# A decoder layer on one core: who makes the rests of the two down weight pieces of the third product

## The reference, cut to what matters

```python
z = rmsnorm(h, norm_mlp[l])                                   # h: 1024 x 1024
h = h + jnp.square(jax.nn.relu(z @ w_up[l])) @ w_down[l]      # w_up 1024 x 4096, w_down 4096 x 1024
return rmsnorm(h, norm_final)
```

## Time and profile before

| | |
|---|---|
| runs, median of 3 | 1497.07 us (1497.02 to 1497.55) |
| profiled execution, its own time | 1496.87 us |
| its span, first to last instruction | 1494.8 us |
| TensorE clock granted, mean | 0.995 |
| busy: PE, DVE, ACT, POOL | 98%, 66%, 35%, 35% |
| a window (seven of them, the last 500 us or so) | 77.6 to 77.7 us |

### The profile page before, as it was taken

The page is one execution under the profiler, slowest core; times in us unless marked ns, Lnnn a source line. Parts: engine busy times, 40 slices in busy tenths (PEclk is TensorE's granted clock), DMA queues, the critical chain, the costliest instruction groups (busy, mean ns, idle before and its releaser), DMA issues.

```text
span 1494.8 us, 20639 instructions
## 1 busy us (share of the span) xinstructions
PE 1465.8 (98%) x7019; PEld 1210.5 (81%) x7019; DVE 981.0 (66%) x1911; ACT 517.9 (35%) x1003; POOL 519.2 (35%) x349
## 2 busy tenths in 40 slices
PE   9999999999999999999999999999999999999995
PEld 8887888888888888888888888878787878787874
DVE  6898564543467527675624788595958586767678
ACT  7422312400122212241101322545444444444455
POOL 4000001245332332004333003273737373646556
PEclk9999999999999999999999999999999999999998
DMA  7225543282111101003542001333333333333333
GB/s 221 99 90 143 144 109 124 72 279 88 57 43 43 43 29 57 29 29 131 179 176 71 1 29 50 120 99 116 103 112 106 104 108 107 108 107 110 107 111 135
DMA packets 150933, 149.02 MB, mean 100 GB/s; under 512 B 19104, under 2 KB 109904, under 8 KB 150864
## 3 DMA queue, kind: packets, MB, share of 16 engines
q1 hardware_dynamic: 118048, 107.00, 23.2%
q10 hardware_dynamic: 32816, 41.12, 8.5%
HBM read 126.58 MB, written 21.50 MB: 99 GB/s over the span
## 4 chain that ended last, share of the span: by engine, by line
PE 84%; DVE 9%; issue 3%; ACT 2%; POOL 1%; ACTq 1%; DMA 0%; DVEq 0%; POOLq 0%
PE acc L799 19%; PE acc L801 19%; PE acc L800 19%; PE aux L800 7%; PE aux L801 7%; PE aux L799 7%; DVE h_ring L2602 1%; DVE h_res L2634 1%; PE aux L1081 1%; PE aux L1074 1%; PE aux L1084 1%; DVE h_sum L2609 1%; PE aux L964 1%; PE aux L958 0%; PE aux L1069 0%
## 5 line engine op out<-in xcount | busy, mean ns | idle before, releaser
L799 PE MATMUL acc<-z_hi,w_hi 128*128 128x512 f32 x448 | 177.2, 396 | 0.6 <-DVE z_lo L1874 0.6
L801 PE MATMUL acc<-z_hi,w_lo 128*128 128x512 f32 x448 | 174.6, 390 | 0.0
L800 PE MATMUL acc<-z_lo,w_hi 128*128 128x512 f32 x448 | 174.5, 390 | 0.0
L799 PE MATMUL acc<-w_hi,z_hi 128*128 128x512 f32 x384 | 164.4, 428 | 0.0
L801 PE MATMUL acc<-w_hi,z_lo 128*128 128x512 f32 x384 | 150.5, 392 | 0.0
L800 PE MATMUL acc<-w_lo,z_hi 128*128 128x512 f32 x384 | 149.6, 390 | 0.0
L663 POOL CAST w_hi<-stage 128x1024 fp32r<-128x1024 f32 x22 | 27.7, 1259 | 344.2 <-PE acc L801 290.0
L650 POOL TENSOR_SCALAR stage<-stage,nm 128x512 f32<-128x512 f32 x48 | 78.3, 1643 | 168.8 <-PE acc L801 86.0
L767 POOL TENSOR_TENSOR t_raw<-t_raw,p_a 128x512 f32<-128x512 f32 x28 | 39.5, 1409 | 262.3 <-DMA p_a<-in_w_up 157.1
L799 PEld LDWEIGHTS acc<-z_hi,w_hi 128*128 128x128 f32 x448 | 84.1, 188 | 19.8 <-issue 1.5
L801 PEld LDWEIGHTS acc<-z_hi,w_lo 128*128 128x128 f32 x448 | 84.1, 188 | 17.9
(11 more groups left out here) (417 smaller groups left out, 3879.7 us busy)
## 6 DMA issues: line engine op xcount, KB each, us to landing
stage<-in_w_in SPq DMA_DIRECT2D x28, 512.0 KB, 4.4
p_a<-in_w_up SPq DMA_DIRECT2D x56, 256.0 KB, 2.8
p_a<-in_w_down SPq DMA_DIRECT2D x56, 256.0 KB, 2.6
gate_dram<-gate_t ACTq DMA_DIRECT2D x32, 256.0 KB, 2.1
p_b<-in_w_up SPq DMA_DIRECT2D x28, 256.0 KB, 2.7
p_b<-in_w_down SPq DMA_DIRECT2D x28, 256.0 KB, 2.7
x_in<-in_x SPq DMA_DIRECT2D x8, 512.0 KB, 6.1
stage<-in_w_in SPq DMA_DIRECT2D x32, 128.0 KB, 2.3
```

What stands on the lines that cost most here:

```text
L799: nc.tensor.matmul(out, s_hi, m_hi_, start=first, stop=False, skip_group_check=partial)
L800: nc.tensor.matmul(out, s_hi, m_lo_, start=False, stop=False, skip_group_check=partial)
L801: return nc.tensor.matmul(out, s_lo, m_hi_, start=False, stop=last, skip_group_check=partial)
```

## The change

VectorE instead of GpSimd makes the rests of pieces 18 and 19 of every window.

```diff
--- before
+++ after
@@ -69,7 +69,7 @@
 N_PROD = len(PRODUCTS)
 PIECES, RING, HRING = 4 * N_PROD, 7, 3
 UP_PIECES = 2 * N_PROD
-V_PIECES = range(3, 18)
+V_PIECES = range(3, 20)
 SUMS = 16
```

## The result

The changed kernel takes 1505.52 us (median of six, 1504.24 to 1506.49) against 1497.16 us for the one before (six, 1496.98 to 1497.55). The ratio is 1.0054, with a 95% interval of 1.0042 to 1.0067: slower by 8.4 us, where 6.5 us (1503.4 us) was predicted. The profiled execution took 1506.17 us, its span is 1504.1 us.

What follows compares the result with a forecast made beforehand. PE, busy 98%, bounds the kernel; only its idle time before piece 18 can change. Chain steps 0.85 + 1.30 - 0.14 - 1.09 = 0.92 us a window, 6.5 in seven: 1496.87 + 6.5 = 1503.4 us, range 1498.0 to 1508.0.

Steps and rivals of the forecast that it cites:

- What PE waits for: Before piece 18, PE idles 1.15 us for DVE's hidden_lo(4), not for the rests that the change moves.
- about 2.0: Sign in the changed kernel: PE's wait before piece 18 in us, instead of 1.15, still ended by hidden_lo(4).
- the slip before piece 17: hidden_lo(3) ends 0.2 us later than PE wants it for piece 17; the wait at piece 18 swallows this.
- Step 1, sum 21: POOL's sum 21 starts earlier, takes its turn behind hidden_s3(1) and ends 1.15 us after it.
- Step 2: DVE's hidden_s1(1) waits for sum 21, ending 0.55 us behind it and 0.97 us later than before.
- Step 4: DVE's rest 18, issued at 1136.24, waits for POOL's rest 20 and is done at 1137.62.
- Steps 5 and 6: POOL's sum 22 goes before hidden_s2(1)'s end; hidden_lo(4) then has no POOL turn ahead and takes 0.69 us.
- The sum: PE starts piece 18 0.92 us later in each window, 6.5 us in seven.
- No gap opens before piece 19: hidden_lo(5) ends by about 1141.2, or 1142.3 with one more POOL turn; PE wants it at 1142.78.
- A: Rival: POOL's operations fall beside add_pair or into DVE's gaps; piece 18 0.58 us earlier per window, 1492.8 us; chance 0.12.
- B: Rival: sum 21 after hidden_lo(3), sum 22 in front of hidden_lo(4); 0.6 us later per window, 1501 us; chance 0.10.
- C: Rival: POOL also gets in front of hidden_lo(4), 1.15 us more per window, 14.5 us in all, 1511.4 us; chance 0.05.

Runs made afterwards that it cites:

- Experiment 4: Kernel before, nothing moved, GpSimd waits with rest 19 and all behind it until hidden_lo(4) is done: 1493.04 us, ratio 0.997.
- Experiment 5: Changed kernel, with GpSimd waiting with sum 21 and all behind it until hidden_lo(4) is done: 1499.08 us, ratio 1.0011 against the kernel before.
- experiment 3: Changed kernel, with GpSimd's sum 21 also waiting for ScalarE's cast 18: 1508.64 us, ratio 1.0074 against the kernel before.
- experiment 1: Kernel before with only rest 18 moved to VectorE, rest 19 left on GpSimd: 1511.73 us, ratio 1.0104.
- experiments 1 to 7: The follow-up kernels, variants of the kernel before or the changed one in moved rests, GpSimd waits or a repeated hidden_lo(4): 1492.81 to 1534.47 us.

## Why the prediction was right

The direction and the term that carries it held, and the mechanism showed step by step:

- *What PE waits for.* `hidden_lo(4)`, not the rests that are moved. Experiment 4 shows it: taking GpSimd out of its way, PE's gap falls from 1.30 to 0.20 us. The two waits put down to POOL's `t_b` in the earlier trace rows went with the others. In the changed kernel the idle time before piece 18 is 1.82 us where "about 2.0" stood: the slip before piece 17 is taken from it.
- *Step 1, sum 21.* Predicted to start behind `hidden_s3(1)`; its data was there 2.77 us after the issue (2.82 expected), and it ends 1.15 us after `hidden_s3(1)`, as worked out.
- *Step 2.* `hidden_s1(1)` predicted at 1.66 us, measured 1.67. PE's slip before piece 17 was predicted at 0.2 us and is 0.25 with the slow matmul behind it; the gap that follows swallows it, as said.
- *Step 4.* Rest 18 predicted at 1.38 us, measured 1.38.
- *Steps 5 and 6.* `hidden_s2(1)` 0.65 and 0.68 us; `hidden_lo(4)` 0.69 and 0.68 us.
- *The sum.* 0.92 us a window predicted, 0.95 measured; 6.5 and 6.7 us in seven. No gap opens before piece 19, as said.

**The term that was missing** is the clock. The prediction priced PE's longer wait at its length alone, and said that a change outside PE can win or lose only PE's idle time. But behind a gap of 2 us the granted clock sometimes falls to half for eight matmuls, 0.2 us lost on each, 1.6 us a time, and this is time in which PE is busy (78.44 instead of 76.79 us in the window). It is in none or one of the six whole windows of the changed kernel's three traces. That fits the spread of the six timed executions, 2.2 us where the kernel before had 0.6 beside them. The rest of the difference is in the early part and isn't the change's. 8.4 us were measured where 6.7 + 1.6 x (0 to 1) + 0 to 1.0 stands.

**The rivals.** A (1492.8 us) asked that sum 21's data land over 1.5 us later than it did; the trace of the changed kernel speaks against it, and its own condition, GpSimd's operations beside the `add_pair` ones, wasn't made in any run. Experiment 5, which takes GpSimd out of the chain by holding it, gives 1499.1: the gap is A's, and a late GpSimd costs the rest behind it. B was priced at 4 us and said to lie in the range; experiment 3, which is close to it, costs 11 us, in good part by the wait before piece 19 that I hadn't worked out. So had the data of sum 21 landed some 1.3 us later, the forecast of 6.5 us would have been 4 to 5 us too low by experiment 3, an estimate: the number leaned on one landing time, and that was read rightly. C's extra turn in front of `hidden_lo(4)` is there in experiment 1, where rest 18 waits less in exchange: 0.56 us more a window than the change (gaps of 2.54 and 1.98 us), not the 1.15 that I had put on it.

The Trainium skill (SBUF — State Buffer, Who interferes with whom) says of the shared pair that the one who issues first holds it for its whole instruction. The ends in every trace here agree, with a blocked VectorE operation 0.55 us behind GpSimd's end and about 1.15 us the other way. The same page's Summary: rules for kernel authors advises to schedule whichever is off the critical path. Experiment 4 is a way to do so, and there it is worth 4.5 us.

## What to carry to other kernels

Moving an operation from GpSimd to VectorE doesn't take GpSimd out of VectorE's way: its next instruction moves up and takes the turn, and the moved one lengthens VectorE's own chain. Find the VectorE operation that TensorE waits for, and hold GpSimd back there with a wait, if what it would do isn't due yet (here one wait, 4.5 us faster, where the move cost 8.4), and hold it no longer than that: experiment 5 held it 6.3 us and lost behind the gap what it had won there. When a chain is worked out turn by turn, go on to the next two places where TensorE could wait, and price each gap of TensorE with the clock that may follow it.

## What the runs showed of the hardware

- Half clock behind a gap, which I had not expected of gaps this short: matmuls 0.43 us apart instead of 0.227. They start 1.3 to 1.5 us after PE resumes behind gaps of 1.9 to 2.5 us, and 0 to 0.8 us after it behind gaps of 4.5 to 4.7 us. In PE's rows that is its 1.2 GHz level in place of 2.4. The two traces of the kernel before have none in twelve whole windows, the three of the changed kernel two in eighteen, each in a different window. The kernel before may not be free of them: beside experiments 1 to 7, four of its 27 executions took 1499.5 to 1500.5 us, none of them traced, and the two longest have a mean granted clock of 0.994 where all others have 0.995 or 0.996. What decides whether a gap is followed by a spell stays open.
- `add_pair`, which reads PSUM and SBUF, ran in 1.13 us steps beside GpSimd in all kernels; no single one took over 1.23 us in any of the twelve traces.
- A VectorE operation with two SBUF inputs that waited for GpSimd ended 0.54 to 0.56 us after GpSimd's operation, in the windows of all twelve traces; a GpSimd one that waited for VectorE ended 1.12 to 1.18 us after it.
